# Prompt attention of a hybrid decoder step, rebuilt: one accumulation for three branches, v stationary, scores formed last in each step

## The reference

```
def nsa_attend(q, gates, qpos, ctx, k_w, v_w, kpos_w):        # 16 heads of 64 in 4 groups
    s_c = einsum('bqghd,bcgd->bqghc', qg, k_c) * scale         # 31 compressed blocks
    p_c = softmax(where(valid_c, s_c, NEG)) * valid_c
    o_c = einsum('bqghc,bcgd->bqghd', p_c, v_c)
    ...
    _, idx = lax.top_k(score, min(N_SELECT, ns))               # 16 wanted, ns = 8 blocks
    ...
    p_s = softmax(where(valid_k, s_s, NEG))                    # selected blocks
    o_s = einsum('bqghn,bgqnd->bqghd', p_s, v_s)
    ...
    p_w = softmax(where(valid_w, s_w, NEG))                    # sliding window of 512
    o_w = einsum('bqghk,bkgd->bqghd', p_w, v_w)
    o = g[..., 0:1] * o_c + g[..., 1:2] * o_s + g[..., 2:3] * o_w
```

## Time and profile before

| | |
|---|---|
| median of three runs | 3580.81 us |
| the profiled execution, and its span in the trace | 3583.95 us, 3582.3 us |
| busy of the span: PE, DVE, ACT, POOL | 3235.1 (90%), 1317.7 (37%), 768.3 (21%), 229.1 us (6%) |
| weight loads on PE (they overlap its products) | 2989.4 us |
| granted clock of PE, mean over the span | 0.879 |
| busy in the 466 us that hold the prompt's attention: PE, DVE, ACT | 398.30, 220.72, 107.02 us |
| granted clock of PE in them | 0.51 |

### The profile page before, as it was taken

The page is one execution under the profiler, slowest core; times in us unless marked ns, Lnnn a source line. Parts: engine busy times, 40 slices in busy tenths (PEclk is TensorE's granted clock), DMA queues, the critical chain, the costliest instruction groups (busy, mean ns, idle before and its releaser), DMA issues.

```text
span 3582.3 us, 52534 instructions
## 1 busy us (share of the span) xinstructions
PE 3235.1 (90%) x20686; PEld 2989.4 (83%) x20686; DVE 1317.7 (37%) x2085; ACT 768.3 (21%) x1183; POOL 229.1 (6%) x334
## 2 busy tenths in 40 slices
PE   7999988989988999988789999878888968799998
PEld 6999977867757999987689999857777744799998
DVE  4323334343444323333143233334444434343232
ACT  3212222212122212121221122212222211121121
POOL 0000021121300000000300000000000012000000
PEclk9999999999998999997989999855555568899999
DMA  2222222332422222232512222400000025112222
GB/s 95 89 73 82 85 94 95 118 119 89 152 94 71 82 82 82 86 104 84 162 47 91 71 82 85 157 16 9 1 0 1 0 88 170 62 65 89 73 83 80
DMA packets 80241, 287.27 MB, mean 80 GB/s; under 512 B 10515, under 2 KB 18883, under 8 KB 79235
## 3 DMA queue, kind: packets, MB, share of 16 engines
q1 hardware_dynamic: 59330, 205.38, 17.0%
q0 software_dynamic: 20800, 80.40, 6.7%
HBM read 260.97 MB, written 33.16 MB: 82 GB/s over the span
## 4 chain that ended last, share of the span: by engine, by line
PE 81%; issue 7%; DVE 5%; DMA 3%; SPq 1%; ACT 1%; POOL 1%; POOLq 0%; DVEq 0%; ACTq 0%
PE ps L426 59%; PE ps L1458 3%; PE ps L623 3%; PE ps L1430 3%; PE ps L1446 2%; PE ps L1189 1%; DMA sample_state<-in_state 1%; PE ps L1693 1%; PE ps L1486 1%; PE ps L1169 1%; SPq L1918 1%; DMA out_state_s<-sample_state 1%; PE ps L672 1%; PE ps L664 1%; DVE rstd L318 1%
## 5 line engine op out<-in xcount | busy, mean ns | idle before, releaser
L301 DVE TENSOR_TENSOR w_low<-w_staged,w_high 128x1024 fp32r<-128x1024 f32 (+1 forms) x334 | 440.8, 1320 | 1082.2 <-ACT w_high L296 1082.2
L296 ACT ACTIVATE w_high<-w_staged 128x1024 fp32r<-128x1024 f32 (+1 forms) x334 | 373.3, 1118 | 1189.3 <-PE ps L426 1043.3
L426 PE MATMUL ps<-xh_f,w_high 128*128 128x288 f32 x2816 | 609.3, 297 | 13.1 <-DVE xl_f L410 13.1
L426 PE MATMUL ps<-xl_f,w_high 128*128 128x288 f32 x2816 | 607.2, 297 | 0.0
L426 PE MATMUL ps<-xh_f,w_low 128*128 128x288 f32 x2816 | 607.0, 297 | 0.0
L426 PEld LDWEIGHTS ps<-xh_f,w_high 128*128 128x128 f32 x2816 | 453.7, 190 | 14.7 <-issue 13.8
L426 PEld LDWEIGHTS ps<-xl_f,w_high 128*128 128x128 f32 x2816 | 454.4, 190 | 0.0
L426 PEld LDWEIGHTS ps<-xh_f,w_low 128*128 128x128 f32 x2816 | 454.0, 189 | 0.0
L426 PE MATMUL ps<-hh,w_high 128*128 128x288 f32 x1408 | 305.3, 298 | 19.3 <-DVE hl L544 19.3
L426 PE MATMUL ps<-hl,w_high 128*128 128x288 f32 x1408 | 304.3, 297 | 0.0
L426 PE MATMUL ps<-hh,w_low 128*128 128x288 f32 x1408 | 303.8, 297 | 0.0
(11 more groups left out here) (361 smaller groups left out, 4275.0 us busy)
## 6 DMA issues: line engine op xcount, KB each, us to landing
w_staged<-in_wa SPq DMA_DIRECT2D x270, 512.0 KB, 3.2
w_staged<-in_wb SPq DMA_DIRECT2D x64, 704.0 KB, 4.1
sample_state<-in_state POOLq DMA_DIRECT2D x32, 512.0 KB, 6.3
out_state_s<-sample_state POOLq DMA_DIRECT2D x32, 512.0 KB, 4.6
cmp_pages<-in_pages_cmp POOLq DMA_DIRECT2D x64, 256.0 KB, 3.3
k_pages<-in_pages_k SPq DMA_DIRECT2D x64, 128.0 KB, 2.1
v_pages<-in_pages_v POOLq DMA_DIRECT2D x64, 128.0 KB, 2.5
k_window<-in_win_k SPq DMA_DIRECT2D x8, 512.0 KB, 4.4
```

The lines of the kernel that those rows point to most:

```text
L296: act.activation(wh[:, slot, 0:size], wf[:, slot, 0:size], ACT.Copy).then_inc(hi_ready, 1)
L301: dve.tensor_tensor(wl[:, slot, 0:size], wf[:, slot, 0:size], wh[:, slot, 0:size].bitcast(F32), ALU.subtract).then_inc(lo_ready, 1)
L426: mm = pe.matmul(ps[:, out + h, 0:HALF], w[:, slot, cols:cols + P], m[:, h * HALF:(h + 1) * HALF], start=(first and n == 0), stop=(last an ...
```

## The change

The new program has 64 steps n in one line, eight for each pair of heads t: i = n % 8 // 2 is the tile of queries, j = n % 2 the branch, and a step holds both groups g at once.

- The compressed blocks of all eight pairs are done at the start, once: 64 score products, one pass of masking, exponential and sums over all of them, 16 turnings, two copies. Their probabilities lie 32 columns apart, so that a turned block of 128 rows holds the four tiles of queries; the values are laid out to match (`vc_by_tile`, `vcr`). The turned compressed probabilities stay until the end, in the tiles of `att_cos_sin` and `stats_broadcast` (`pct`).
- The causal mask is rounded and added by PE, as a product of the unit matrix with the mask (`unit_and_causal`, `cm_r`), after the three score products of both groups. DVE adds no mask.
- DVE multiplies the exponentials by gate over sum before PE turns them (`scaled`). The turning waits for that (`att_probs_ready`) where it waited for ACT.
- A value product has 64 columns of v stationary and the 128 turned probabilities moving, and writes the output already turned: group 0 to the lower 64 partitions of its bank, group 1 to the upper. Compressed, selected and window branches of a tile add up in one accumulation in PSUM. The output is split into `ah` (ACT) and `al` (DVE) from there; `ot`, its additions and its turnings are gone.
- There are no loops: each engine's program is written out for all 64 steps. POOL splits q as before and no longer copies it whole; it clears and fills `vc_by_tile` once, and its last wait is for the last value product, since one of the tiles with compressed probabilities is used again by the samples.

```diff
@@ tiles
-                    pr = sb(s2, "probs", [P, 2, 1024])
-                    pc = sb(s2, "probs_cmp", [P, 8, NC_P])
-                    prt = sb(s2, "probs_T", [P, 2, 1024])
-                    ot = sb(s2, "o_by_token", [P, 4, P])
+                    cm_r = sb(s2, "unit_and_causal", [P, 2, P], F32R)
+                    pr = sb(s2, "probs", [P, 2, 2, PT])
+                    prt = sb(s2, "probs_T", [P, 2, 2, PT])
+                    vcr = sb(s2, "vc_by_tile", [P, 256])
...
+        pct = [over_resting(atab, P, KT), over_resting(rb_rows, P, KT)]
+        pc = prt.rearrange("p a g c -> p (a g c)")
...
+        def part(n):
+            return n // 8, n % 8 // 2, n % 2
...
+        def half(g):
+            return slice(DH * g, DH * (g + 1))
@@ att_pe
+            def scores(n):
+                t, i, j = part(n)
+                past(pe, a_exp, n - 1)
...
+                for m, (qq, kk) in enumerate(((qh, kh), (qh, kl), (ql, kh))):
+                    for g in range(2):
+                        pe.matmul(ps[:, 2 * j + g, 0:w], qq[half(g), t % 2, i * P:(i + 1) * P],
+                                  kk[half(g), k, 0:w], start=(m == 0), stop=False, skip_group_check=True)
+                for g in range(2):
+                    mm = pe.matmul(ps[:, 2 * j + g, i * P:w], cm_r[:, 0, :], cm_r[:, 1, :], start=False,
+                                   stop=True, skip_group_check=True)
+                mm.then_inc(a_s, 1)
+            def turned(n):
+                t, i, j = part(n)
+                pe.wait_ge(a_p, n + 1)
+                past(pe, a_ptv, n)
+                past(pe, a_pta, n)
+                for g in range(2):
+                    for k in range(i + 1):
+                        mm = pe.transpose(ps[:, 4 + g, k * P:(k + 1) * P], pr[:, j, g, k * P:(k + 1) * P], ident)
+                mm.then_inc(a_t, 1)
+            def values(n):
+                t, i, j = part(n)
+                pe.wait_ge(a_ptv, n + 1)
+                pe.wait_ge(a_pta, n + 1)
...
+                def to(g):
+                    return ps[half(g), 6 + t % 2, i * P:(i + 1) * P]
...
+                if j == 0:
+                    rows = slice(32 * i, 32 * i + 32)
+                    for g in range(2):
+                        pe.matmul(to(g), vcr[rows, group(g):group(g) + DH], pct[g][rows, t, :], start=True,
+                                  stop=False, skip_group_check=True)
+                for k in range(i + 1):
+                    for g in range(2):
+                        c0 = 256 * j + group(g)
+                        mm = pe.matmul(to(g), v_tok[:, k, c0:c0 + DH], prt[:, n % 2, g, k * P:(k + 1) * P],
+                                       start=False, stop=(j == 1 and k == i), skip_group_check=True)
+                mm.then_inc(a_v, 1)
...
+            for n in range(N_ATT):
+                turned(n)
+                if n:
+                    values(n - 1)
+                if n + 2 < N_ATT:
+                    scores(n + 2)
+            values(N_ATT - 1)
@@ att_act
+            def high(t):
+                act.wait_ge(a_v, 8 * t + 8)
+                act.activation(ah[:, t, 0:PT], ps[:, 6 + t % 2, :], ACT.Copy).then_inc(a_high, 1)
...
+            for n in range(N_ATT):
+                taken(n)
+                if n + 2 < N_ATT:
+                    probs(n + 2)
+                if n >= 8 and n % 8 == 0:
+                    high(n // 8 - 1)
@@ att_dve
+            def maxima(n):
+                t, i, j = part(n)
+                dve.wait_ge(a_s, n + 1)
+                cv.link(dve.tensor_reduce(stat[:, j, 0, :], ps[:, 2 * j:2 * j + 2, 0:P * (i + 1)], AX_X, ALU.max))
+                dve.tensor_scalar(stat[:, j, 1, :], stat[:, j, 0, :], -SCALE, None, ALU.mult).then_inc(a_mx, 1)
+            def scaled(n):
+                t, i, j = part(n)
+                dve.wait_ge(a_exp, n + 1)
+                cv.link(dve.reciprocal(ls[:, n % 2, :], sums[:, n % 4, :]))
+                gate = gt[:, i, 6 * t + 1 + j:6 * t + 5 + j:3]
+                cv.link(dve.tensor_tensor(ls[:, n % 2, :], ls[:, n % 2, :], gate, ALU.mult))
+                for g in range(2):
+                    row = pr[:, j, g, 0:P * (i + 1)]
+                    ins = dve.tensor_scalar(row, row, ls[:, n % 2, g:g + 1], None, ALU.mult)
...
+                        ins.then_inc(a_p, 1)
+            def taken(n):
+                t, i, j = part(n)
+                dve.wait_ge(a_t, n + 1)
+                past(dve, a_v, n - 1)
+                dve.tensor_copy(prt[:, n % 2, 0, 0:P * (i + 1)], ps[:, 4, 0:P * (i + 1)]).then_inc(a_ptv, 1)
...
+            for n in range(N_ATT):
+                if n + 2 < N_ATT:
+                    maxima(n + 2)
+                taken(n)
+                if n + 1 < N_ATT:
+                    scaled(n + 1)
+                if n >= 8 and n % 8 == 0:
+                    low(n // 8 - 1)
@@ att_pool
+            pool.wait_ge(a_v, N_ATT)
```

364 lines of the change are left out of this document (135 added, 229 removed).

## The result

The changed kernel takes 3597.02 us (median of 20 runs, 3582.47 to 3603.69), the kernel before 3583.06 (20 runs). The ratio is 1.0038, with a 95% interval of 1.0028 to 1.0049: 14 us slower, where 12 were forecast. The profiled execution has a span of 3589.3 us.

What follows compares the result with a forecast made beforehand. PE bounds the stage now (busy 398.30 of 466 us). Steps of PE's 4.36 plus DVE's 2.64 in series, 441, front 33 and end 5 give 479 against 463; less 4 for the clock, 12 us slower: 3593, range 3558 to 3632.

Steps and rivals of the forecast that it cites:

- The order of steps: Attention steps: PE's and DVE's legs in series, since the next turning waits for scaling behind maxima; 55 in 100.
- mask, to DVE's start: PE's two mask products: 0.21 to the second, 0.39 to its end, 0.04 to DVE; 0.64 us a step.
- DVE's leg, to PE's start: DVE's reduction, copy, reciprocal, gates, two scalings and the way back to PE: 2.64 us a step, between 2.3 and 3.0.
- step: One of 64 attention steps: PE's leg 4.36 plus DVE's leg 2.64, 7.00 us.
- Changes of shape: PE's array: 0.13 us charged after the scores and for two changes in every second step's compressed products.
- The clock: PE's clock in the attention: a few spells at the higher level, 4 us off the sum.
- the 3.56 for each of the last two steps: End of the attention: the last two steps lack scores and maxima, 3.56 us each, making 441 for all steps.
- the 3610: Whole kernel's time, us, if turnings to values and values to scores also cost 0.13 each by the skill's rule.
- Of the rivals, the clock: Value products and scores filling both array halves raise the clock and pay for the wait; 3555 at 40%; chance 23.
- Value products and scores pair: PE runs two groups' products at once; unpaired, values cost up to +69 us, scores +56; slow-products rival 3650 to 3660, chance 19.
- Rounded score products of 128 columns: PE's narrow scores: no row shows their price, 0 to +10 us, lower taken; slow narrow products rival 3621, within chance 19.
- DVE's round nowhere got ahead: Rival: PE and DVE not put in turn, DVE's round getting ahead, PE's leg alone counts; 3435 us, chance 3.

Runs made afterwards that it cites:

- The first two edits: Changed kernel with DVE scaling first and its maxima last, 3402.81 us; changed kernel with PE's scores first, 3366.48 us.
- the next two: Changed kernel with PE's value products last, after the scores, 3506.89 us; changed kernel without DVE's scaling of the probabilities, 3530.34 us.
- The run with more changes: Changed kernel with score pairs and halves of the value products interleaved on PE, so the array's shape changes 2.6 times more a step: 3646.19 us.
- the runs that broke the turns: Changed kernel with DVE scaling first (3402.81 us), PE's scores first (3366.48), or scores first with mask on DVE (3370.22), ACT taking both turned blocks (3329.61), or both (3347.86).
- the runs by group: Changed kernel with all of group 0's products before group 1's: value products so ordered, 3608.61 us; score products so ordered, 3598.37 us.

## Why the prediction was right

The order of steps was the one forecast: DVE's maxima wait for the last product of a step, the scaling stands behind them, the next turning waits for the scaling. The first two edits show it from both engines, the next two in size. Term by term, with means over the first 62 steps, from one row's start to the next (turning, value product, score product, mask, DVE's reduction, turning):

| term | predicted, us | measured, us |
|---|---|---|
| front, once | 33 | 33.5 (2409.30 to 2442.83) |
| turnings, a step | 1.11 | 1.22 (1.26 at the lower clock) |
| value and compressed products | 1.08 + 0.35 | 1.50 (1.58) |
| scores | 1.18 | 1.12 (1.15) |
| mask, to DVE's start | 0.64 | 0.68 (0.72) |
| DVE's leg, to PE's start | 2.64 | 2.54 (2.55) |
| step | 7.00 | 7.05 (7.25) |
| stage | 479, less 4 for the clock | 481.1 |

The figure in brackets is the mean over the eight steps of the fifth turn, nearly all of it at the lower level, for which the prediction's terms were meant; one of the eight has 0.65 us of a hold by POOL in it (last section). The sum hit closer than its terms, which is in part luck: errors cancelled.

- **Changes of shape, too cheap.** The sum charged 0.13 after the scores and in the compressed products, and let the other changes pass. The single starts of the trace have 0.350 from the last turning to the first product of the values (2661.747 to 2662.097) and 0.351 from the last value product to the first score product (2664.273 to 2664.624), against 0.213 between alike ones: 0.14 each, twice a step, 17 us over 62 steps. The run with more changes shows that it is the change, not the waits at the head of these products, and that the gap is not the whole of its cost.
- **The clock, too cheap.** At the granted clock of 0.50 the eight steps of a turn take 6.12, 5.59, 6.12, 7.30, 7.83, 9.01, 7.40 and 8.05 us. With all steps from the second on at these lengths, and POOL's holds as they fell, they would take 442 us; they took 433. The higher clock gave 9 us, where 4 were taken. The last step of the first turn took 7.19 us, with the clock up behind its wide products, the like steps of the third to sixth turns 8.05.
- **DVE's leg, too dear.** 2.54 a step against 2.64 is 6 us over 62 steps, though 4 us of POOL's holds are in it, for which the sum had no term.

Two smaller terms were off as well. The mask's two products start 0.27 apart (2657.008 and 2657.279), not 0.21, so that the mask took 0.72 at the lower level in place of 0.64. And the 3.56 for each of the last two steps doesn't come out of the other terms (7.00 less 1.18, 0.64 and 0.94 is 4.24; the first of the two took 3.94), about 1 us in the sum.

By the rule of the Trainium skill that the prediction set beside its sum (TensorEngine Tiling (Array Packing), section Key Properties: a change of tiling mode drains TensorE) turnings and value products are dearer by those 17 us. The trace agrees, with 0.14 a change where the prediction had put 0.13 beside the rule, so the rule was right about these terms; the 3610 that it gave still lies farther from 3597 than 3593, since the clock and DVE's leg were too dear in the same sum.

Of the rivals, the clock was real but small while PE waited; the runs that broke the turns show how large it gets (0.75 to 0.89). Value products and scores pair, and the price of 69 us for value products that don't was not tested. Rounded score products of 128 columns, for which no row stood, took the lower bound (pairs of them start 0.21 apart, 2656.45 and 2656.67). DVE's round nowhere got ahead.

## What to carry to other kernels

When two in-order engines work in a pipeline, write down for each what it does last before the signal and what the other does before it signals back; the work between these points is in series, whatever else is free, and what no dependence holds there can move behind the signal, on either engine. Fewer busy microseconds (398 to 306 on PE, 221 to 174 on DVE) can be a longer stage. Try the other order of each queue before judging a rewrite: here two blocks of PE's program, exchanged, turned 1.0038 into 0.9387. And when a few us are at stake, compare steps of the same kind at the same granted clock before the difference is put down to the edit.

## What the runs showed of the hardware

By the spacing of its starts, PE begins a product of the other half of the array ahead of up to three instructions that stand before it in its program (the runs by group, above).

A tiny operation of DVE was held by POOL. In six of the 64 steps the scaling of two maxima, 0.17 us long, took 0.82, and it ended when POOL's subtraction ended (2650.28 + 0.82 = 2651.10; below, 2649.82 + 1.26 = 2651.08):

```profile
2649.12 0.61 POOL L1628 CAST q_pair_h<-q_T 128x512 fp32r<-128x512 f32 x1 [56.01 <-PE ps L1443]
2649.82 1.26 POOL L1629 TENSOR_TENSOR q_pair_l<-q_T,q_pair_h 128x512 fp32r<-128x512 f32 x1
```

To test it, POOL's split waits for one signal more:

```diff
                 past(pool, a_s, 8 * (t - 1))
+                past(pool, a_t, 8 * (t - 1) - 1)
```

> The changed kernel with POOL's split of q begun a little later: it also waits for the turning of the next step, so that its 2 us lie in the stretch in which DVE waits for PE's scores. Theory (DVE's tiny scaling of the maxima, 0.82 in place of 0.17 in six steps of the changed trace, was held until POOL's subtraction ended: 2650.28 + 0.82 against 2649.82 + 1.26): all six become 0.17, the stage is 6 x 0.65 = 4 us shorter, 3593, hardly to be told from 3597. Rival (DVE's row is long for another reason, the step's width say, since it was always step 5 of a turn): six long rows stay, at the same steps. Rival 2 (the hold moves): other DVE rows in those turns grow by up to 1 us.

All six became 0.17, no scaling of the probabilities grew (0.49 at most, as before), and the time is 3587.81, where 3593 was forecast. DVE's timeline in the same turn of that kernel, with the tiny scaling and the wait for PE's next scores, and then POOL's, which now falls into that wait:

```profile
2647.21 0.17 DVE L1554 TENSOR_SCALAR att_stats<-att_stats 128x2 f32<-128x2 f32 x1
...
2653.77 0.42 DVE L1553 TENSOR_REDUCE att_stats<-ps 128x2 f32<-128x256 f32 x1 [4.74 <-PE ps L1443]
```

```profile
2651.91 1.27 POOL L1630 TENSOR_TENSOR q_pair_l<-q_T,q_pair_h 128x512 fp32r<-128x512 f32 x1
```

So the hold was POOL's, and the step's width is not the reason. With the mask on DVE, where POOL's subtraction stood earlier beside these six operations, they took 0.35 to 0.36 and again ended with it (2651.46 + 0.35 = 2651.81; 2650.52 + 1.27 = 2651.79). The Trainium skill says the like (SBUF — State Buffer, section Who interferes with whom): DVE and POOL share a pair of ports under an exclusive lock, which a tensor_scalar can need.

With POOL's split later the stage is 16 us shorter, 4 of them the rows. Steps of the same kind at a granted clock of 0.50 are otherwise as long as in the change, within 0.01; the other 12 came with the clock, 0.61 against 0.56, and why the shift raised it stays open.
